# Three edits to the split order of a two-layer fp32 transformer kernel: who splits the branch weight tiles, when the last down product's second tile is split, where the first map scores stand

## What is computed

```
# block 1 (first_block)
mixed = gate_a * (o_a @ w_branch_a) + gate_b * (o_b @ w_branch_b)
h = h + mixed @ w_out
h = h + (silu(hn @ w_ffn_gate) * (hn @ w_ffn_up)) @ w_ffn_down
# block 2 (mixer_block, differential attention and windowed attention)
attn = softmax(s1) - lam * softmax(s2)          # two score maps per head, 4 heads
merged = sigmoid(ga) * (y_a @ w_ba) + sigmoid(gb) * (y_b @ w_bb)
h = h + merged @ w_o
h = h + swiglu(rms_norm_2(h), w_gate, w_up, w_down)
```

## Time and profile before

| what | us |
|---|---|
| median of 3 runs | 1500.18 |
| the profiled execution's own time | 1499.58 |
| its span, first to last instruction | 1497.9 |
| TensorE busy in the span | 1477.7 |
| VectorE busy | 957.0 |
| ScalarE busy | 605.1 |
| GpSimd busy | 221.2 |

### The profile page before, as it was taken

One profiled execution on the slowest core, in us unless ns is written; L12 is line 12 of the kernel. 1 busy time (PEld: TensorE's weight loads), 2 busy tenths in 40 slices (PEclk: granted clock), 3 DMA queues, 4 the chain that ended last, 5 costly groups with the idle time before them and its releaser, 6 DMA issues.

```text
span 1497.9 us, 21903 instructions
## 1 busy us (share of the span) xinstructions
PE 1477.7 (99%) x8042; PEld 1233.0 (82%) x8042; DVE 957.0 (64%) x1707; ACT 605.1 (40%) x1061; POOL 221.2 (15%) x194
## 2 busy tenths in 40 slices
PE   8999999999999999999999999999999999999998
PEld 7867776878788888898898777777787888888987
DVE  6668897565795587377854372424667855873865
ACT  5235436534443243244511374444344433432434
POOL 2013324340000000000003663322400000000000
PEclk9999999999999999999999999999999999999999
DMA  7624320033333333332323202121333333333322
GB/s 174 152 65 146 117 57 1 23 104 99 98 99 99 101 97 99 98 104 71 107 85 84 56 2 85 57 64 36 102 95 99 99 99 112 89 95 98 113 70 100
DMA packets 250309, 132.99 MB, mean 89 GB/s; under 512 B 21225, under 2 KB 247653, under 8 KB 250222
## 3 DMA queue, kind: packets, MB, share of 16 engines
q1 hardware_dynamic: 247998, 123.92, 29.2%
q0 software_dynamic: 2144, 7.77, 1.8%
q10 hardware_dynamic: 80, 0.14, 0.0%
HBM read 129.67 MB, written 6.38 MB: 91 GB/s over the span
## 4 chain that ended last, share of the span: by engine, by line
PE 91%; DVE 5%; DMA 1%; issue 1%; ACT 1%; POOL 0%; SPq 0%; DVEq 0%; ACTq 0%
PE psL L2050 50%; PE psS L2073 12%; PE psL L2236 11%; PE psS L2050 5%; PE psT L2245 2%; PE psL L2371 1%; PE psS L2541 1%; PE psL L2496 1%; PE psS L2344 1%; PE psS L2519 1%; PE psS L2475 1%; DVE acc L1479 1%; PE psS L2286 1%; DVE st L1478 1%; PE psS L2476 0%
## 5 line engine op out<-in xcount | busy, mean ns | idle before, releaser
L775 ACT ACTIVATE wh<-stage 128x1024 fp32r<-128x1024 f32 (+3 forms) x232 | 225.4, 971 | 366.2 <-PE psL L2050 260.0
L2050 PE MATMUL psL<-hn,wh 128*128 128x512 f32 x1104 | 347.9, 397 | 0.4 <-DVE ft L1733 0.4
L2050 PEld LDWEIGHTS psL<-hn,wh 128*128 128x128 f32 x1104 | 204.8, 188 | 50.3 <-issue 3.7
L1208 DVE TENSOR_TENSOR wl<-stage,wh 128x1024 fp32r<-128x1024 f32 (+1 forms) x157 | 187.6, 1195 | 78.9 <-ACT wh L775 78.5
L2050 PE MATMUL psL<-hn,wl 128*128 128x512 f32 x552 | 217.1, 393 | 0.0
L2050 PE MATMUL psL<-hid,wh 128*128 128x512 f32 x680 | 209.6, 390 | 1.4 <-DVE wl L1208 1.4
L636 POOL TENSOR_TENSOR wl<-stage,wh 128x1024 fp32r<-128x1024 f32 (+2 forms) x75 | 140.0, 1867 | 278.5 <-ACT wh L775 278.5
L2236 PE MATMUL psL<-hn,wh 128*128 128x512 f32 x496 | 166.9, 418 | 2.2 <-DVE tmp L1468 2.0
L2050 PEld LDWEIGHTS psL<-hid,wh 128*128 128x128 f32 x680 | 127.4, 188 | 28.9 <-DVE wl L1208 2.2
L2050 PE MATMUL psL<-hid,wl 128*128 128x512 f32 x340 | 132.3, 389 | 0.0
L2050 PEld LDWEIGHTS psL<-hn,wl 128*128 128x128 f32 x552 | 103.8, 188 | 23.5
(11 more groups left out here) (438 smaller groups left out, 2644.3 us busy)
## 6 DMA issues: line engine op xcount, KB each, us to landing
stage<-in_w_in SPq DMA_DIRECT2D x54, 512.0 KB, 3.8
stage<-in_w_ffn_gate SPq DMA_DIRECT2D x22, 512.0 KB, 3.8
stage<-in_w_ffn_up SPq DMA_DIRECT2D x22, 512.0 KB, 3.8
stage<-in_w_ff_gate SPq DMA_DIRECT2D x22, 512.0 KB, 3.8
stage<-in_w_ff_up SPq DMA_DIRECT2D x22, 512.0 KB, 3.8
stage<-in_w_out SPq DMA_DIRECT2D x16, 512.0 KB, 4.0
stage<-in_w_ffn_down SPq DMA_DIRECT2D x16, 512.0 KB, 4.0
stage<-in_w_ff_down SPq DMA_DIRECT2D x16, 512.0 KB, 4.1
```

The source lines that it names most:

```text
L775: act.activation(wh[:, b, 0:n], stage[:, b, 0:n], ACT.Copy).then_inc(hi[b], 1)
L1208: v.tensor_tensor(wl[:, b, 0:n], stage[:, b, 0:n], wh[:, b, 0:n].bitcast(F32), ALU.subtract).then_inc(lo[b], 1)
L2050: ins = pe.matmul(dst, w[:, b, k * P:(k + 1) * P], x[:, part, k, c0:c1], start=k + n == 0, stop=k == kc - 1 and n == 2)
```

## The change

It does three things. (1) `br1` and `br2` leave `POOL_LOW`: GpSimd no longer runs `lows("br1")` and `lows("br2")`, and the `low` and `low_next` calls that stand in VectorE's `branches` become real instructions; VectorE's low part of tile (0, 0) stands ahead of `heads_low`. (2) The high and the low part of tile (0, 1) of `dn1c` and `dn2c` move to the end of `swiglu(l, 2)`, ahead of the last `inner_high` and `inner_low`. (3) The score maps of j = 0 are issued inside the last product of `qb2`, ahead of its fifth block of input rows, and VectorE scales that product out in step j = 1 of df in place of before df.

```diff
-POOL_LOW = ("iq1", "aq1", "uq1", "gates1", "br1", "qa2", "qb2", "gates2", "br2")
+POOL_LOW = ("iq1", "aq1", "uq1", "gates1", "qa2", "qb2", "gates2")
...
# gpsimd
-            lows("br1")
...
-            lows("br2")
# scalar, swiglu
                     if not last:
                         sum_high(n + 1, 1)
                         second_high(name, i + 2)
+                    elif part == 2:
+                        high(f"dn{l}c", 0, 1)
                     inner_high(i + 1, f0)
...
-            high(name, 0, 1)
             for i in range(PAIRS[name]):
                 pair1(i, i == PAIRS[name] - 1)
...
             for i in range(last):
-                if i == 0:
-                    high(name, i, 1)
                 chunk2(i, 0)
# vector
+            low("br1", 0, 0)
             heads_low(1, oB)
...
                     if not last:
                         second_low(name, i + 2)
+                    elif part == 2:
+                        low(f"dn{l}c", 0, 1)
                     inner_low(i + 1, f0)
...
             clear_squares()
-            low("dn1c", 0, 1)
             meta_low(2)
...
-                    take_scaled(name, i, 1, dst[:, 2 * i + 1, :], R, QSCALE)
+                    if i == 0 or name == "qa2":
+                        take_scaled(name, i, 1, dst[:, 2 * i + 1, :], R, QSCALE)
...
             for j in range(16 + 5):
+                if j == 1:
+                    take_scaled("qb2", 1, 1, qbT[:, 3, :], R, QSCALE)
...
+            low("br2", 0, 0)
             heads_low(2, oA, subg[:])
...
             def last_part(i):
-                low("dn2c", i, 1)
+                if i:
+                    low("dn2c", i, 1)
# tensor
-            products("qb2", hn)
-
-            pe.wait_ge(nat_taken, 3)
             p = ph["df"]
+            def map_scores(j):
...
+            product("qb2", 0, 0, hn)
+            product("qb2", 0, 1, hn)
+            product("qb2", 1, 0, hn)
+            product("qb2", 1, 1, hn, between={(0, 4): lambda: map_scores(0)})
             for j in range(16 + 4):
+                if 0 < j < 16:
+                    map_scores(j)
```

More of the change, by code:

```diff
@@ L2461, in _ @@
             products("qa2", hn, first=1)
-            products("qb2", hn)
-            pe.wait_ge(nat_taken, 3)
             p = ph["df"]
-            for j in range(16 + 4):
[L2467 to L2476, removed]
+            def map_scores(j):
+                i, h = divmod(j, 4)
+                if j == 0:
+                    pe.wait_ge(nat_taken, 3)
+                for m in range(2):
+                    u = 2 * j + m
+                    r = slice(m * HD, (m + 1) * HD)
+                    if u >= 2:
+                        pe.wait_ge(p["neg"], u - 1)
+                    q = qaT[r, h, i * P:(i + 1) * P]
+                    pe.matmul(psS[:, 2 * m, 0:NKEY // 2], q, kaT[r, h, 0:NKEY // 2], start=True, stop=True)
+                    pe.matmul(psS[:, 2 * m + 1, 0:NKEY // 2], q, kaT[r, h, NKEY // 2:NKEY], start=True, stop=True).then_inc(p["s"], 1)
+            product("qb2", 0, 0, hn)
+            product("qb2", 0, 1, hn)
+            product("qb2", 1, 0, hn)
+            product("qb2", 1, 1, hn, between={(0, 4): lambda: map_scores(0)})
+            for j in range(16 + 4):
+                if 0 < j < 16:
+                    map_scores(j)
                 for n, u, i in turns_at(j - 2, 4):
```

## The result

The changed kernel takes 1513.72 us, the median of 4 runs (1512.41 to 1515.48), against 1499.72 for the kernel before in the same job (4 runs, 1499.02 to 1501.77). The ratio is 1.0090, 95% interval 1.0077 to 1.0103: slower by 14.0 us, where 13.5 were predicted. The profiled execution took 1514.3 us, with a span of 1512.6 and a mean granted clock of 0.996.

A forecast was written before the change was run, and what follows sets the result against it. TensorE is busy 1477.7 of 1497.9 us, so only waits going or coming can move the time. The terms 18.0-1.85+0.15-1.8-1.0 = +13.5 us gave a forecast of 1513.4 us, range 1508.0 to 1519.5.

The forecast's parts named there:

- The chain of a pair: Branch pairs: VectorE's steps before the split of tile (i+1, 1) make TensorE wait until N+4.05; a pair lasts 6.90 us.
- the shortening of the sum from 1.70 to 0.69 us: VectorE's sum in each branch pair takes 0.69 us instead of 1.70 once no GpSimd split runs beside it.
- Rival (b): The sum in each branch pair stays at 1.70 us, each pair 1.0 us longer, +14: 1527.5 us; chance 0.04.
- There TensorE doesn't wait at all: Branch pair timeline before the change: TensorE has no wait there; no size given.
- that it ran on a slower engine cost nothing: Branch tiles before the change: GpSimd's low part was hidden with 0.5 us to spare.
- Edit 1 net: Branch splits moved to VectorE: +9.0 us a layer, +18.0 for both, with -1.85 for both at the starts of `out`.
- Rival (a): Branch splits stay hidden on VectorE; only the other two edits and the `out` starts count: 1495.7 us; chance 0.06.
- Rival (c): SP's loads of the next branch tiles come late too, 0.3 us a pair, +4: 1517.5 us; chance 0.12.
- Rival (d): A smaller stall in the branch pairs, some 0.3 us each, about the time of now, 1500 us; chance 0.03.
- Ahead of `br2`: VectorE's new low part of tile (0, 0) pushes back the first `heads_low`; +0.15 us for both layers, bounds 0 and 0.5.
- Edit 2: Second down tile of `dn1c` and `dn2c`: TensorE's wait for its low part goes; -1.8 us for both, bounds -1.4 and -2.0.
- Edit 3: Start of df: first score maps made inside the `qb2` product, first transposes start earlier; -1.0 us, bounds -0.5 and -1.3.

The follow-up runs named there:

- experiment 6: The changed kernel with the slot 1 tiles of `br1` and `br2` split by GpSimd again, slot 0 left to VectorE; 1497.81 us.
- experiment 2: The changed kernel with VectorE's split of tile (i+1, 1) moved directly behind the sum, ahead of its wait for ScalarE; 1494.49 us.
- experiment 3: The kernel before with only the second down tile's splits of `dn1c` and `dn2c` moved earlier; 1498.72 us.
- experiment 4: The kernel before with only the score maps of j = 0 issued inside the last product of `qb2`; 1499.47 us.
- experiments 2 and 7: The latter: experiment 2's kernel with the score maps of j = 1 also issued inside the last product of `qb2`; 1494.19 us.
- experiment 5: The changed kernel with VectorE's split of tile (i, 1) one instruction later, behind the gating of (i, 0); 1531.79 us.

## Why the prediction was right, and where its terms were off

**The chain of a pair** was right to a few hundredths of a microsecond. With N the moment at which the product behind (i, 1) starts, 317.49 in the pair above, by TensorE's own row:

| step | predicted | measured |
|---|---|---|
| gating of product (i, 1) starts | N+0.32 | N+0.32 |
| sum starts | N+1.11 | N+1.12 |
| ScalarE's part starts | N+1.92 | N+1.93 |
| subtraction starts | N+2.70 | N+2.71 |
| the split starts | N+3.31 | N+3.32 |
| the split ends | N+4.00 | N+4.01 |
| TensorE goes on | N+4.05 | N+4.06 |
| a pair lasts | 6.90 | 6.92 |

The step that carried most risk was the shortening of the sum from 1.70 to 0.69 us. It was read from the one instance at the last pair, where no GpSimd split ran, and experiment 6 shows that the reading was right. Rival (b) is out.

**One reading was too simple.** "There TensorE doesn't wait at all" holds for the pair shown, but not for all: the gaps of 0.5 us booked as "issue" in three of the pairs of `br1` were waits for GpSimd's split of slot 0 (experiment 2). So "that it ran on a slower engine cost nothing" is true of slot 1 only: the split on GpSimd made the sum long, and the long sum made slot 0 late. It did no harm to the forecast, since that took the mean of seven pairs, 5.62 us, gaps included. A forecast for experiment 2 from "hidden" alone would have missed 2.5 us.

**Edit 1 net**: +8.22 and +8.07 us in the two stages, and 0.15 us less than that in each once the restart is counted, so some 8.07 and 7.92; 9.0 less 0.92 were predicted for each. Rival (a) is out as a description of this change, but experiment 2 shows that it was a true description of the engine choice: with the split ahead of the wait for ScalarE, the branch splits stay hidden on VectorE, and the time is 1494.5, close to the 1495.7 priced for it. That closeness has luck in it: the price held nothing for the 2.5 us of the waits at slot 0. The prediction had named that condition ("only if VectorE didn't wait for ScalarE's part of the sum"). The Trainium skill, "GPSIMD Engine Reference", section 4.1, was right about the engine and says nothing of the order in which it is to do the work. **Rival (c)**, late loads: in the pairs of `br1` ScalarE waits for TensorE's slot (27.8 us in 14 places) and for VectorE's sum (7.3 in 7), and its one wait for a transfer, 0.5 us, is for a tile of `out`; the pair's 6.92 us against 6.90 leaves nothing for it. Out. **Rival (d)** is out by the pair's length. **Ahead of `br2`** 0.23 us instead of 0.15 for both.

**Edit 2** gained 0.86 us at the second tile of `dn1c` and 0.85 at that of `dn2c`, and with the restarts 1.04 and 0.95: 2.0 for the 1.8 predicted, at the end of its bounds. Alone it measured -1.1 by the medians, with -1.8 inside its interval, and 2.0 by its trace (experiment 3).

**Edit 3** is the term that was mis-sized: -1.0 predicted, -0.65 by the traces of the kernel after and of experiment 4; its own runs can't tell the two apart. The step that failed is "VectorE reads the two maps of j = 1 from 851.0 at some 0.7 us each", in the working of edit 3: it took TensorE's scores to be at VectorE's disposal about 0.85 us after they start and the wait for L1485 to be mostly gone. VectorE reads a map 1.19 to 1.20 us after its scores start, in both kernels, so that the reading came at what would be 851.4 and not at 851.0 (860.00 less the lag of 8.58), and after the change one wait of 0.80 us remains. What went was the short second one and a part of the way to the first transposes.

**What was not in the sum**: the start-up, +0.85 us, and the clock. Behind the 16 one-column matmuls of the norm's sums the clock fell in the kernel after. The window of the kernel before (columns as above):

```profile
750.00:760.00 10.00, 9.65 (x70) 8.57 (x69) 6.97 (x12) 1.06 (x1) 1.04 (x2) 1.00 0.20 58
```

and of the kernel after:

```profile
750.00:760.00 10.00, 9.76 (x64) 9.27 (x64) 7.57 (x32) 1.06 (x1) 0.00 (x0) 0.83 0.19 55
```

From 752.4 to 755.8 after, a single 264-column matmul goes at a pitch of 0.22 us where before it is 0.12, and the lag grows from 7.65 to 9.19 us, by 1.54. The stage came out only 0.28 longer, and two things took the rest. One is a wait that the kernel before has a little later and the kernel after has not:

```profile
750.48 1.13 PE L2115 MATMUL psT<-diag,ones 128*128 128x512 f32 x2 [0.35 <-DVE tmp L1250]
```

TensorE needs there what VectorE makes of the norm's sums in a line of small instructions, which takes 5.73 us from its first one to the next weight split in both traces. TensorE came later, and found it ready:

```profile
759.16 1.02 PE L2119 MATMUL psT<-diag,ones 128*128 128x512 f32 x2
```

With its restart that wait was worth 0.61 us (the lag is 9.19 ahead of it and 8.58 behind). The other is edit 3, 0.65. The fall isn't the change's doing: experiments 2 and 7 show 0.83 at the same place, and the six others show 1.00. So one profiled execution of 1512.6 us holds a microsecond or two that the next may not have, and the closeness of 13.5 and 14.0 is better than the method. What was shown to the hundredth is the pair; the rest of the sum is right to about 1 us.

## What to carry to other kernels

When work moves to another in-order engine, read what stands ahead of it there, not only how fast it is: on a slot with one buffer the time from the end of a product to the ready tile must fit under the one product that covers it, and here a wait for a third engine lay in between. The wait itself is the place for the moved work: put directly ahead of it, the same instruction cost nothing (a pair of 5.44 us), put behind it 1.5 us a pair (6.92), 1.3 more than on GpSimd (5.62). And a small idle time booked as "issue" at the start of a product can be a wait: look at when the operand that it needs was ready.

## What the runs showed of the hardware that was not expected

- **With more waiting in each pair the clock fell.** With 1.78 us of waiting in each pair of 7.5 us (experiment 5) the granted clock fell to its lower level, 1.2 GHz, five times in 16 pairs, for some 3 us each; with 1.18 us in each pair of 6.9 us (the kernel after) the windows from 300 to 350 and from 1050 to 1100 us all read 1.00. The falls came while TensorE was working, 1.3 to 1.4 us behind the end of a wait. So a wait's price isn't constant: the 0.61 us more in each of 14 pairs and the two new waits cost 11.8 us as waits, and 6.6 us more through the clock. What decides between the two cases no run here separates, and the waiting as the cause of the falls is argued from these two kernels alone.
- **The clock at the one-column matmuls.** At the 16 matmuls with one column each, 1.95 us long, or within some 1 us behind them, the clock fell in three of the ten traces (the kernel after, experiments 2 and 7) and not in the others, with the same instructions. At the start of df, where TensorE waits 0.80 and 0.2 us, it fell in one of ten (experiment 3).
- **A wait behind a fall of the clock hides part of it.** Of the 1.54 us that the fall cost in the kernel after, 0.61 came back at once, because TensorE would have waited for VectorE there.
- **From scores to read.** A map of two 64-row, 264-column fp32 matmuls, sharing TensorE with the other map, is read by VectorE 1.19 to 1.20 us after the first of them starts, in the kernels before and after and in experiment 4.
